# Expert weight chunks of a 33-item MoE loop: all twelve low parts subtracted on VectorE, gated activations transposed after down chunks 10 and 11

## The reference

```
logits = h @ w_router + b_router;  top 4 of 32 experts, gates = softmax(top 4)
hgu = ragged_dot(xs, w_gate_up) + b_gate_up          # per expert 1024 x 2048
x_glu = min(hgu[::2], 7);  x_lin = clip(hgu[1::2], -7, 7)
act = x_glu * sigmoid(1.702 * x_glu) * (x_lin + 1)
out = ragged_dot(act, w_down) + b_down               # per expert 1024 x 1024
out * gate, summed per token
```

## Time and profile before

| | |
|---|---|
| median of 3 runs | 2700.23 us (2699.74 to 2705.22) |
| the profiled execution | 2706.93 us |
| its span in the trace | 2705.1 us |
| PE, DVE, ACT, POOL busy | 2422.9, 1776.5, 1244.4, 969.9 us |
| DMA | 555.04 MB, 205 GB/s over the span |
| the loop over items, PE's first bias product to its last transpose | 493.6 to 1771.9 us of the span, 32 passes |

### The profile page before, as it was taken

The page is one execution under the profiler, slowest core; times in us unless marked ns, Lnnn a source line. Parts: engine busy times, 40 slices in busy tenths (PEclk is TensorE's granted clock), DMA queues, the critical chain, the costliest instruction groups (busy, mean ns, idle before and its releaser), DMA issues.

```text
span 2705.1 us, 29243 instructions
## 1 busy us (share of the span) xinstructions
PE 2422.9 (90%) x10384; PEld 1863.4 (69%) x10384; DVE 1776.5 (66%) x1641; ACT 1244.4 (46%) x1214; POOL 969.9 (36%) x389
## 2 busy tenths in 40 slices
PE   6989886999999999999999999949998799899996
PEld 3647654777777777777777777737676587778875
DVE  3524436898898989898898989852556625532423
ACT  1112303666666666666666666622335732321320
POOL 1030034566566657556656655720110001100001
PEclk9979975999999999999999999969998899899998
DMA  7000142899999999999899999772211022222220
GB/s 267 12 36 1 55 174 72 310 346 330 334 365 316 356 345 342 342 336 354 321 354 342 339 347 345 248 241 74 78 43 63 32 96 107 79 92 96 105 79 31
DMA packets 141554, 555.04 MB, mean 205 GB/s; under 512 B 11200, under 2 KB 12352, under 8 KB 124528
## 3 DMA queue, kind: packets, MB, share of 16 engines
q1 hardware_dynamic: 129968, 512.46, 51.1%
q0 software_dynamic: 10368, 37.49, 5.4%
q10 hardware_dynamic: 1152, 4.19, 0.4%
HBM read 525.80 MB, written 28.31 MB: 205 GB/s over the span
## 4 chain that ended last, share of the span: by engine, by line
PE 63%; DVE 24%; issue 8%; ACT 4%; DMA 1%; POOL 1%; DVEq 0%; SPq 0%; POOLq 0%; ACTq 0%
PE PS L377 59%; DVE low L1779 14%; PE PS L662 2%; DVE act L1785 2%; DVE act_parts L1774 1%; DVE act L1789 1%; DVE act L1502 1%; ACT act L1413 1%; ACT act L1290 1%; DVE act L1505 1%; POOL act L2073 1%; DVE st L1490 1%; PE PS L531 1%; DVE small L1949 1%; DVE act L1947 1%
## 5 line engine op out<-in xcount | busy, mean ns | idle before, releaser
L377 PE MATMUL PS<-act_parts 128*128 128x512 f32 (+1 forms) x3300 | 1075.4, 402 | 36.0 <-DVE low L1779 26.2
L1779 DVE TENSOR_TENSOR low<-ring,act_parts 128x2048 fp32r<-128x2048 f32 x297 | 843.8, 2885 | 69.9 <-ACT act_parts L1283 69.9
L377 PEld LDWEIGHTS PS<-act_parts 128*128 128x128 f32 (+1 forms) x3300 | 625.2, 191 | 211.0 <-DVE low L1779 44.3
L2177 POOL TENSOR_TENSOR low<-ring,act_parts 128x2048 fp32r<-128x2048 f32 x99 | 575.3, 5811 | 459.5 <-ACT act_parts L1283 459.4
L1283 ACT ACTIVATE act_parts<-ring 128x2048 fp32r<-128x2048 f32 x396 | 731.4, 1910 | 10.9 <-PE PS L377 10.6
L377 PE MATMUL PS<-low,act_parts 128*128 128x512 f32 x1584 | 625.3, 395 | 0.0
L377 PE MATMUL PS<-act_parts,ring_parts 128*128 128x512 f32 x1216 | 381.4, 403 | 6.5 <-DVE act_parts L2001 3.7
L377 PEld LDWEIGHTS PS<-low,act_parts 128*128 128x128 f32 x1584 | 303.0, 191 | 58.7
L1861 DVE TENSOR_TENSOR ring_parts<-ring,ring_parts 128x4096 fp32r<-128x4096 f32 x30 | 132.7, 4423 | 231.7 <-ACT ring_parts L1352 231.6
L377 PEld LDWEIGHTS PS<-act_parts,ring_parts 128*128 128x128 f32 x1216 | 235.0, 193 | 70.8 <-issue 12.1
L2073 POOL TENSOR_TENSOR act<-act 128x1024 f32<-128x1024 f32 (+1 forms) x21 | 53.4, 2542 | 622.8 <-DVE act L1505 622.8
(11 more groups left out here) (219 smaller groups left out, 2017.5 us busy)
## 6 DMA issues: line engine op xcount, KB each, us to landing
ring<-w_gate_up SPq DMA_DIRECT2D x264, 1024.0 KB, 9.6
ring<-w_down SPq DMA_DIRECT2D x132, 1024.0 KB, 6.9
ring<-w_ff SPq DMA_DIRECT2D x16, 2048.0 KB, 7.7
ring<-w_in SPq DMA_DIRECT2D x12, 2048.0 KB, 8.5
ring<-w_o SPq DMA_DIRECT2D x1, 4096.0 KB, 22.7
ring<-w_out SPq DMA_DIRECT2D x2, 2048.0 KB, 8.1
acc_d<-act SPq DMA_DIRECT2D x5, 512.0 KB, 2.6
act<-x SPq DMA_DIRECT2D x4, 512.0 KB, 5.1
```

The lines of the kernel that those rows point to most:

```text
L377: return eng.matmul(o, lhsT, rhs, start=first, stop=last, **kw)
L1779: tt(W1lo[c], W1[c], W1hi[c % CS].bitcast(F32), ALU.subtract).then_inc(low_sem(c), 1)
L2177: tt(W1lo[c], W1[c], W1hi[c % CS].bitcast(F32), ALU.subtract).then_inc(low_sem(c), 1)
```

## The change

DVE makes the low parts of all twelve chunks, in the order of the chunks, and POOL makes none. Chunk 3 comes between chunk 2 and the second half of the activation, chunk 7 behind chunk 6, chunk 11 behind chunk 10. The semaphores `low_dve` and `low_pool` become one, `low`, with the counts of `high`. On PE, `turn_gated` of the first half moves from behind chunk 9 to behind chunk 10; that of the second half stays behind chunk 11. The number of instructions is the same as before; only the engine of 99 subtractions and the place of 4 transposes in each pass change. ACT and SP are not edited.

```diff
@@ PE
                     for c in range(4 * hh, 4 * hh + 4):
-                        eng.wait_ge(low_sem(c), count_low(i, c))
+                        eng.wait_ge(sem["low"], count_high(i, c))
...
                 for hh in range(2):
                     eng.wait_ge(sem[f"aT_low{hh}"], i)
                     for c in range(8 + 2 * hh, 10 + 2 * hh):
-                        eng.wait_ge(low_sem(c), count_low(i, c, not turning))
+                        eng.wait_ge(sem["low"], count_high(i, c, not turning))
...
                         ins.then_inc(sem["down_used"], 1)
-                    if turning:
-                        turn_gated(i, hh)
+                        if turning and c == 10:
+                            turn_gated(i, 0)
+                if turning:
+                    turn_gated(i, 1)
@@ DVE
             def chunk_low(i, c, last=False):
                 eng.wait_ge(sem["high"], count_high(i, c, last))
-                tt(W1lo[c], W1[c], W1hi[c % CS].bitcast(F32), ALU.subtract).then_inc(low_sem(c), 1)
+                tt(W1lo[c], W1[c], W1hi[c % CS].bitcast(F32), ALU.subtract).then_inc(sem["low"], 1)
...
                 act_low(i, 0)
                 chunk_low(i, 2)
+                chunk_low(i, 3)
                 act_low(i, 1)
-                for c in (4, 5, 6):
+                for c in range(4, 8):
                     chunk_low(i, c)
                 swiglu(i, 0)
-                for c in (8, 9, 10):
+                for c in range(8, CH):
                     chunk_low(i, c)
                 swiglu(i, 1)
                 rows_low(i + 1)
...
-            for c in (0, 1, 2, 4, 5, 6):
+            for c in range(8):
                 chunk_low(0, c)
...
-            for c in (8, 9, 10):
+            for c in range(8, CH):
                 chunk_low(n_extra + E, c, last=True)
@@ POOL
             def item(i, second=False):
-                chunk_low(i, 3)
                 next_rows(i)
                 if not second:
                     add_product(i)
-                chunk_low(i, 7)
                 next_select(i)
-                chunk_low(i, 11)
```

More of the change, by code:

```diff
@@ L310, in build @@
         block = ctx.enter_context(nc.Block())
-        BY_POOL = (3, 7, 11)
-        BY_DVE = tuple(c for c in range(CH) if c not in BY_POOL)
         def count_high(i, c, last=False):
             return c + 1 if isinstance(i, int) and i == 0 else CH * i + (c - 11 if last else c - 3)
[L319 to L330, removed]
         where = {}
@@ L2174, in _ @@
             eng.memset(maskb[0:DH, S - DH:S], NEG).then_inc(signal("mask_ready"), 1)
-            def chunk_low(i, c, last=False):
-                eng.wait_ge(sem["high"], count_high(i, c, last))
-                tt(W1lo[c], W1[c], W1hi[c % CS].bitcast(F32), ALU.subtract).then_inc(low_sem(c), 1)
             def add_product(i):
@@ L2200, in item @@
                     add_product(i)
-                chunk_low(i, 7)
                 next_select(i)
-                chunk_low(i, 11)
             eng.wait_ge(*past("places_listed", 1))
-            chunk_low(0, 3)
             next_rows(0)
-            chunk_low(0, 7)
             next_select(0)
@@ L2218, in _ @@
             add_product(n_extra + E)
-            chunk_low(n_extra + E, 11, last=True)
             add_product(n_extra + (E + 1))
```

## The result

The changed kernel takes 2591.09 us, the median of 4 runs (2588.18 to 2594.9), beside 2701.65 us for the kernel before on the same chip (4 runs). The ratio is 0.9586, with a 95% interval of 0.9574 to 0.9597: 111 us faster. The forecast was 2606 us, with a range from 2593 to 2648.

What follows compares the result with a forecast made beforehand. The prediction took a loop between DVE and PE as the bound; 32 passes falling from 39.94 to 37.0 us (PE 36.9, DMA 0.1) save 94 us, taking the median from 2700.23 to 2606 us, range 2593 to 2648.

Steps and rivals of the forecast that it cites:

- The cause: Item loop: DVE is late because it takes turns with POOL's subtractions; without them its pass falls from 36.68 to 33.7 us.
- The waits: PE's waits in a pass, 0.93 us ahead of down chunk 9 and 2.25 ahead of the transposes, both go.
- half-clock stretches: Where PE resumes after its wait, the clock drops for part of a window; none expected without waits.
- The transposes: Moving the first half's transposes behind down chunk 10 costs nothing, covered by about 5 us of slack on ACT.
- The pass without waits: Item loop: PE needs 36.90 us a pass without its two waits; with 0.1 for DMA, 37.0 us.
- bracket: PE's wait as the timeline shows it: 0.93 us ahead of down chunk 9, 2.25 ahead of the transposes.
- DMA: Loads in the item loop: 36.4 to 37.5 us of work a pass, the next bound beside PE, adding 0.1 us.
- idle windows: Sign against a DMA bound: between 1092 and 1094 the queues are nearly empty, share 0.03, loads waiting for places.
- A: Rival: DMA becomes the loop's bound at 37.6 to 38.8 us a pass, 2648 us at 38.3; chance 0.18.
- B: Rival: the new order leaves PE a wait of 1 to 2 us a pass, 2638 to 2670 us; chance 0.08.
- C: Rival: DMA already bounds the loop and PE's waits only mirror it, so time stays 2700 us; chance 0.03.
- D: Rival: ACT or loads stretch DVE's subtractions, so its pass becomes 45.3 us and the kernel 2873 us; chance 0.03.

Runs made afterwards that it cites:

- e1: The changed kernel with the first half's transposes back behind down chunk 9, so only the subtractions move; 2590.88 us, ratio 0.9592 to the kernel before.
- e3: The changed kernel with GpSimd doing four 128 x 512 additions nobody waits for at each of its three former subtraction places; 2844.88 us.
- e5: The changed kernel with GpSimd doing four 128 x 512 memsets, which only write SBUF, at each of its three former subtraction places; 2587.29 us.
- e2: The kernel before with only the first half's transposes moved behind down chunk 10, GpSimd keeping its three chunks; 2735.41 us, ratio 1.0124.
- e4: The changed kernel without the low x high product of the down projection, 16 of 144 chunk matmuls a pass; 2504.7 us.
- e6: The changed kernel with GpSimd keeping the subtraction of chunk 3 in each pass; 2594.51 us, ratio 0.9594 to the kernel before.
- e7: The changed kernel with GpSimd keeping the subtractions of chunks 7 and 11 in each pass; 2611.68 us, ratio 0.9632 to the kernel before.

## Why the prediction was right, and where it was wrong

**The cause.** Right. DVE was the late one, and it was late because its two-input instructions and GpSimd's subtractions took turns. The forecast had 2.24 us for a chunk and 33.7 of work a pass; it is 2.29 and 33.05. The 33.7 started from one pass of 36.68, and the three of the earlier trace rows have 35.5 on the mean. e1 shows that moving the subtractions alone brings the whole gain, and e3 and e5 show the contention apart from everything else in the change.

**The waits.** Right. Both waits of the earlier trace rows are gone, `xT_low` comes at 27.5 us as worked out, and the half-clock stretches went with the waits: the clock is 1.00 in the whole window, where it was 0.96 in the middle pass of the earlier trace rows.

**The transposes.** Priced at nothing, and e1 shows nothing. The 2.4 us that I had for the old place were right to the tenth. What I didn't see is that the same edit alone makes the kernel slower (e2).

**The pass without waits: the step that failed.** The prediction took 40.08 - 0.93 - 2.25 = 36.90 us for PE's work and the busy time of 36.63 for its lower end, and added 0.1 for DMA. Measured: 36.35. Over 32 passes 0.65 us is 21 us. The first pass gave back 2.0 (38.36 us, with the clock at 0.94), and the pass of item 0, which was priced at nothing, took 1.7 us more than before in this execution (36.5 against 34.7; in the traces of the experiments it takes 34.7 to 36.4). That leaves 17 us, beside the 16.5 by which 2591.1 lies under the forecast, if that is taken from the newer median of before (2701.65 - 94 = 2607.6). That two small misses went against the large one was luck.

The 0.55 us was in the rows of before. The timeline of PE in the pass of the earlier trace rows, around its two waits:

```profile
1041.51 0.61 PE L377 MATMUL PS<-act_parts 128*128 128x512 f32 x2
...
1043.39 0.39 PE L377 MATMUL PS<-low,act_parts 128*128 128x512 f32 x1
...
1045.45 0.61 PE L377 MATMUL PS<-act_parts 128*128 128x512 f32 x2
...
1048.82 0.48 PE L377 MATMUL PS<-act_parts 128*128 128x512 f32 x1
```

The last pair ahead of chunk 9 starts at 1041.51 and 1041.74, so the next one was due at 1041.97, and came at 1043.05: 1.08 us late, where the bracket says 0.93. The last pair ahead of the transposes starts at 1045.45 and 1045.68; they were due at 1045.91 and came at 1048.31, 2.40 late, where the bracket says 2.25. And the first ones after a wait are slow: four transposes took 0.51 us to the next matmul (1048.31 to 1048.82), and 0.39 in the changed kernel (1032.43 to 1032.82); the matmul of 1043.05 took 0.34 to the next one, where 0.23 is usual. The four pieces, 0.15, 0.15, 0.12 and 0.11, are 0.53 of the 0.55 us. A bracket counts from the modelled end of the last matmul, which lies 0.15 us after the moment at which the next could have started. Busy time has the same fault: the pass of 37.80 us has one wait, of 1.17 ahead of the transposes, and 36.63 - 0.15 - 0.12 = 36.36 is the pass that was measured.

**DMA.** Wrong in size, though it cost only the 0.1. The 36.4 to 37.5 us that the prediction has for the work of DMA in a pass took the share of busy time for work. The changed kernel moves the same bytes in 36.35 us at a share of 1.01, and e4 in 34.08 at 1.03. So share times length is not the work: it came to 38.1 us for a pass before, and to 35.1 in e4 for the same bytes. What else the share counts, no run here shows. The idle windows of the earlier trace rows were the better witness.

**The rivals.** A, DMA at 37.6 us or more, is out: 370 GB/s over 1080 us, 400 in e4. The Trainium skill, DMA: Bandwidth & Descriptors, section Where 436 GB/s comes from, has about 358 GB/s as the limit of a core for such transfers. The 370 and 400 GB/s measured here, with one core at work, are above it, and the measurement decides. B, a wait left by the order, did not come. C, no change, and D, slower, are refuted by the result.

## What to carry to other kernels

Two engines that take turns are not two engines. Before giving part of a DVE stream of two-input SBUF operations to GpSimd, look in the trace for operations of the same shape with different durations, and add the stretch to the price of the offload. How large it is depends on where the turns fall, so an edit of the order elsewhere (e2) can change it, and a mean from one order doesn't hold in another (e6, e7).

To find what a loop costs without its waits, count from start to start against an undisturbed stretch, not busy time and not brackets. And don't take a DMA share near 1 for a bound while nobody waits for a load: here 0.99 at 370 GB/s was none.

## What was not expected of the hardware

- Moving four transposes by one chunk made the kernel 1.2% slower while GpSimd shared the work (e2), with a clock of 0.96 in place of 0.99 in the loop, and changed nothing without it (e1).
- Twelve additions of 128 x 512 on GpSimd, for nobody, raised DVE's work from 33.05 to 44.25 us a pass and the pass by 8 us (e3); twelve memsets changed neither (e5).
- A full DMA share, 0.99 to 1.01, at 370 GB/s had room for 400 (e4).
- e7 ran at 2611 to 2616 us three times and at 2589 once; what decides between the two stays open.
